# Sparse attention on one core: a split wait of the values, the first exponential ahead of the next head's high part, and the compressed coefficient behind the last maximum

## The chip, the cores and the metric

The kernel runs on one core of a Trainium2 chip. The metric is the device time of one execution in microseconds (us). A core has five engines with a queue each, which run at the same time and are ordered only by semaphores: PE (matrix products), ACT (activations), DVE and POOL (elementwise work) and SP (here only transfers).

## The reference

The program computes two layers on 512 tokens of width 1024: latent attention (16 heads), then native sparse attention (16 heads in 4 groups, key width 96, value width 64). The change lies in the second layer's attention. With 8 key blocks of 64 tokens and up to 16 selected, every valid block is selected, so the selected branch and the window branch are both causal attention over all 512 tokens, each with its own keys and values, and the compressed branch has 31 keys.

```python
s_c = jnp.einsum('btghd,bngd->bghtn', qc, k_cmp, preferred_element_type=jnp.float32) * scale
p_c = masked_softmax(s_c, cmp_end[None, :] <= t[:, None])
o_c = jnp.einsum('bghtn,bngd->btghd', p_c.astype(v_cmp.dtype), v_cmp)
...
p_s = masked_softmax(s_s, (key_tok <= t[None, None, :, None])[:, :, None])
o_s = jnp.einsum('bghtk,bgtkd->btghd', p_s.astype(v_g.dtype), v_g)
...
p_w = masked_softmax(s_w, m_w)
o_w = jnp.einsum('bghtk,bkgd->btghd', p_w.astype(vb.dtype), vb)
return gc[..., 0:1] * o_c + gc[..., 1:2] * o_s + gc[..., 2:3] * o_w
...
o = jnp.moveaxis(o, 0, 1).reshape(B, S, NSA_HEADS * DV) * jax.nn.silu(z)
return o @ w_out
```

## The kernel before

Every engine has an order written out by hand. The second layer's attention is `sparse_attention`; its `tensor`, `scalar`, `gpsimd` and `vector` functions each run a loop over the 16 heads `n`. Float32 operands are kept as a high and a low part in float16, so a score takes three products.

A head goes through the engines as follows. PE transposes its queries (`turn_q`, L456) into `x_bank`. ACT copies the high part out (`high`, L679) and DVE subtracts it for the low part (`low`, L808). A first, rough score (`first_scores`, L470, six units `u` of tile and branch) goes to DVE, which adds the causal band and takes row maxima (`maximum`, L819). When all six are there, PE turns the maxima into a row (`turn_max`, L478) and ACT writes that row under the queries (`max_row`, L696), so that the exact scores come out with the maximum subtracted. The exact scores are again in six units: `small_terms` (L488, L489), `large_term` (L497, it needs the row), and the causal `mask` (L504). They lie in three banks in turn, so that unit k needs the exponentials of unit k-3. `exponential` on ACT makes two activations of each unit, float32 (L688) and float16 (L691). POOL's `rest` (L776) makes the low float16 part of the probabilities. `values` (L575, L576) multiplies probabilities and values of the head before, in four query tiles `i`. DVE's `leave` (L855, L856, L859) scales what came out, tiles 0 to 2 and then tile 3, and raises `o_left` after each; POOL's `mix` adds the branches.

The compressed branch runs beside this: `compressed_scores` (L540, L541) into `x_bank`, `compressed_read` (L827, L829) on DVE, which frees `x_bank` (`c_left`), `compressed_exponential` (L721) on ACT, `turn_compressed` (L548) and `compressed_values` (L555) on PE, `compressed_turned` (L847), `compressed_coef` (L840, L841) and `compressed_leave` (L867) on DVE. POOL's weight parts (`w_low_part`) and ACT's (`w_high_part`, L708) for the output product are put at the ends of heads 1 to 4.

PE works in head n at `compressed_scores(n)`, `turn_max(n)`, the six score units of n, and, spread between them, `first_scores` of n+1 and `values` of n-1. In the last head `turn_o` (L587, transposes of the mixed output) takes the place of `first_scores`, and then comes the output product.

Of the kernel before, what the change touches and what calls it, by code (L numbers as in the profile page):

```python
# [26 lines left out]
NT = SEQ // P  # L27
# [74 lines left out]
def trunk(nc, x, positions, inv_freq, norm_g, mla_w_in, mla_g_cq, mla_w_uq, mla_g_ckv, mla_w_ukv,  # L102
          mla_g_q, mla_g_k, mla_w_out, nsa_w_in, nsa_g_q, nsa_g_k, nsa_pe_k, nsa_w1_k, nsa_w2_k,
          nsa_pe_v, nsa_w1_v, nsa_w2_v, nsa_w_out, out):
    with ExitStack() as whole:
# [64 lines left out]
        with ExitStack() as layer:  # L170
            z_sb = at_slab("z_sb", 0, [P, NT, ZZ])
            with ExitStack() as ctx:
# [191 lines left out]
                def sparse_attention():  # L364
# [80 lines left out]
                    def tensor(pe):  # L445
# [53 lines left out]
                        def mask(n, u):  # L499

                            j, branches = block_of[u]
                            nb, left = len(branches), left_of(j)
                            dst = score_bank[(U * n + u) % 3][:, 0:nb * left].rearrange("p (b c) -> p b c", b=nb)[:, :, 0:P]
                            nc.tensor.matmul(dst, causal, identb[:, :].unsqueeze(1).to_broadcast([P, nb, P]), start=False,  # L504
                                             stop=True).then_inc(s_done, 1)
# [9 lines left out]
                        def start_scores(n):  # L515

                            if n == 0:
                                pe.wait_ge(n_left, NT * NIN)
                            for u in range(2):
                                k = U * n + u  # L520
                                if k >= 3:
                                    pe.wait_ge(exp_done, k - 2)
                                small_terms(n, u, 0, u)
                            if n + 1 < H:
                                turn_q(n + 1)
                            pe.wait_ge(m_in, n + 1)
                            if n == 0:
                                pe.wait_ge(rows_set, 1)
                            for u in range(2):
                                large_term(n, u, 0, u)  # L530
                            for u in range(2):
                                mask(n, u)

                        def compressed_scores(n):
                            a = n % 2
# [22 lines left out]
                        def values(n, i, branches=(0, 1)):  # L558

                            pe.wait_ge(sub_done, U * n + (2, 4, 5, 6)[i])  # L560
                            if n and i == 0:
                                pe.wait_ge(o_left, 2 * n)
                            if n == H - 1 and i == NT - 1:
                                pe.wait_ge(cv_left, H)
                            if n == 0 and i == 0:
                                pe.wait_ge(v_step, V_REST)
                                pe.wait_ge(rows_set, 3)
                            for b in branches:
                                dst = o_most[:, i, b, :] if i < 3 else o_last[:, b, :]
                                for j in range(i + 1):  # L570
                                    at = at_of[j, b] + (i - j) * P
                                    v = v16(b, j)[:, n // HPG * PIECES:(n // HPG + 1) * PIECES]
                                    for p in (p1, p2):
                                        block = p[n % 2][:, at:at + P]
                                        nc.tensor.matmul(dst, block, v[:, 0:DV1], start=j == 0 and p is p1, stop=False)  # L575
                                        last = nc.tensor.matmul(dst[:, 0:DV], block, v[:, DV1:PIECES], start=False,  # L576
                                                                stop=j == i and p is p2)
                            if i == NT - 1 and branches[-1] == 1:
                                last.then_inc(pv_done, 1)
# [51 lines left out]
                        def attend():  # L631

                            for n in range(H):
# [11 lines left out]
                                start_scores(n)  # L645
                                scores(n, 2)
                                mask(n, 2)
                                beside(0)
                                if n:
                                    values(n - 1, 0)  # L650
                                beside(1)
                                scores(n, 3)
                                mask(n, 3)
                                if n:
                                    values(n - 1, 1)
                                beside(2)
                                scores(n, 4)
                                mask(n, 4)
                                beside(3)
                                if n:  # L660
                                    values(n - 1, 2)
# [14 lines left out]
                    def scalar(act):  # L676
# [48 lines left out]
                        def attend():  # L725
# [3 lines left out]
                            for n in range(H):  # L729
                                max_row(n)  # L730
                                if n == 0:
                                    act.wait_ge(v_step, V_REST)
                                if n + 1 < H:
                                    high(n + 1)
                                exponential(n, 0)
                                exponential(n, 1)
                                if n + 1 == H:
                                    o_high(0)
# [64 lines left out]
                    def vector(dve):  # L803
# [88 lines left out]
                        for n in range(H):  # L892
# [17 lines left out]
                            compressed_turned(n)  # L910
                            if more:
                                maximum(n + 1, 4)
                            compressed_coef(n)
                            if more:
                                maximum(n + 1, 5)
                            compressed_leave(n)
                        leave(H - 2)
                        for k in (4, 5, 6):
# [1540 lines left out]
```

## Time and profile before

| | us |
|---|---|
| median of 3 runs | 896.91 |
| lowest, highest | 895.51, 898.35 |
| the profiled execution | 897.27 |
| its span | 895.4 |
| PE busy in the span | 868.1 |
| DVE busy | 564.0 |
| ACT busy | 513.6 |
| POOL busy | 506.7 |

The granted TensorE clock is full over the whole span. The 16 heads of the sparse attention lie between about 689 and 843 us of the span. Busy time of PE is that of overlapping matmuls, so the space between the starts of two neighbours tells more there than a duration does.

### The profile page before, as it was taken

What the parts mean: (1) busy time and instruction counts of PE and PEld (TensorE: products, weight loads), DVE (VectorE), ACT (ScalarE), POOL (GpSimd) and SP (SyncE); (2) the same over time, 40 slices, a digit from 0 to 9 for tenths busy, and PEclk for the clock granted to TensorE, in tenths of its full rate; (3) what the DMA queues carried; (4) which work ended last, traced back from release to release, by engine and by line L of the source; (5) the groups of instructions that cost most, each with busy time, mean ns of one, the idle gap of its engine ahead of it and who ended that gap; (6) DMA issues with size and microseconds to landing.
All of it is one profiled execution on the core that took longest, in us unless ns stands there. A gap on an engine that the chain in (4) does not pass through costs nothing.

```text
span 895.4 us, 18024 instructions
## 1 busy us (share of the span) xinstructions
PE 868.1 (97%) x6553; PEld 754.7 (84%) x6553; DVE 564.0 (63%) x1628; ACT 513.6 (57%) x1232; POOL 506.7 (57%) x697
## 2 busy tenths in 40 slices
PE   6999998999999999999999999999998999999998
PEld 5999998999999999888888887788876677777786
DVE  4898887887788878321111123587697788888521
ACT  5456666877777777432233323334435999989620
POOL 2000428988888886244346334476683697777631
PEclk9999999999999999999999999999999999999999
DMA  6322313101110110222246221223222001000011
GB/s 210 127 95 95 112 60 98 45 19 52 39 52 27 37 51 11 96 59 83 91 120 142 91 93 48 94 94 91 64 88 94 2 3 49 3 2 3 1 48 48
DMA packets 39330, 59.02 MB, mean 66 GB/s; under 512 B 8757, under 2 KB 22346, under 8 KB 39242
## 3 DMA queue, kind: packets, MB, share of 16 engines
q1 hardware_dynamic: 39200, 57.85, 20.8%
q8 instruction: 53, 0.87, 0.4%
q14 instruction: 35, 0.29, 0.1%
q10 hardware_dynamic: 42, 0.01, 0.0%
HBM read 55.63 MB, written 2.10 MB: 64 GB/s over the span
## 4 chain that ended last, share of the span: by engine, by line
PE 77%; DVE 13%; issue 4%; ACT 4%; POOL 1%; DMA 1%; ACTq 0%; DVEq 0%; POOLq 0%
PE bank L97 17%; PE bank L98 17%; PE bank L99 17%; PE bank L1229 4%; PE bank L1218 2%; PE bank L488 2%; DVE qs L2334 2%; PE bank L497 2%; PE bank L575 2%; DVE w_lo L2058 2%; PE bank L489 2%; PE bank L470 1%; PE bank L1190 1%; PE bank L1191 1%; PE bank L576 1%
## 5 line engine op out<-in xcount | busy, mean ns | idle before, releaser
L1930 POOL TENSOR_TENSOR w_lo<-w_raw,w_hi 128x2048 fp32r<-128x2048 f32 (+1 forms) x26 | 118.4, 4552 | 147.7 <-ACT w_hi L1652 147.6
L97 PE MATMUL bank<-w_hi,h_hi 128*128 128x512 f32 (+3 forms) x472 | 171.1, 362 | 1.3 <-DVE h_lo L1978 1.0
L99 PE MATMUL bank<-w_hi,h_lo 128*128 128x512 f32 (+3 forms) x472 | 166.6, 353 | 0.0
L98 PE MATMUL bank<-w_lo,h_hi 128*128 128x512 f32 (+3 forms) x472 | 166.5, 353 | 0.0
L776 POOL TENSOR_TENSOR p<-kvr,p 128x512 f16<-128x512 f32 (+1 forms) x96 | 88.3, 939 | 37.0 <-ACT p L691 35.8
L97 PEld LDWEIGHTS bank<-w_hi,h_hi 128*128 128x128 f32 x472 | 88.8, 188 | 14.2 <-issue 2.8
L99 PEld LDWEIGHTS bank<-w_hi,h_lo 128*128 128x128 f32 x472 | 88.7, 188 | 11.5
L98 PEld LDWEIGHTS bank<-w_lo,h_hi 128*128 128x128 f32 x472 | 88.9, 188 | 10.0
L1652 ACT ACTIVATE w_hi<-w_raw 128x2048 fp32r<-128x2048 f32 (+1 forms) x26 | 49.1, 1890 | 76.7 <-PE bank L99 76.7
L97 PE MATMUL bank<-w_hi,o_hi 128*128 128x512 f32 x192 | 77.6, 404 | 0.0
L97 PE MATMUL bank<-w_hi,c_hi 128*128 128x256 f32 (+1 forms) x224 | 75.8, 338 | 1.1 <-DVE qn L2144 1.1
L98 PE MATMUL bank<-w_lo,o_hi 128*128 128x512 f32 x192 | 75.8, 395 | 0.0
L99 PE MATMUL bank<-w_hi,o_lo 128*128 128x512 f32 x192 | 75.7, 394 | 0.0
L98 PE MATMUL bank<-w_lo,c_hi 128*128 128x256 f32 (+1 forms) x224 | 68.3, 305 | 0.0
L99 PE MATMUL bank<-w_hi,c_lo 128*128 128x256 f32 (+1 forms) x224 | 68.3, 305 | 0.0
L819 DVE CUSTOM_DVE_ANT_0 scored<-bank,band 128x128 f32<-128x128 f32 (+3 forms) x128 | 58.7, 486 | 10.8 <-PE bank L470 9.8
L688 ACT ACTIVATE kvr<-bank,g_cols 128x512 f32<-128x512 f32 (+1 forms) x96 | 61.2, 638 | 0.9 <-PE bank L504 0.8
L691 ACT ACTIVATE p<-bank,g_cols 128x512 f16<-128x512 f32 (+1 forms) x96 | 61.6, 642 | 0.0
L1598 ACT ACTIVATE qkT_hi<-bank 128x512 fp32r<-128x512 f32 x64 | 38.4, 600 | 27.6 <-PE bank L1191 27.5
L575 PE MATMUL bank<-kv,p 128*128 128x65 f16 x640 | 49.6, 192 | 2.2 <-DVE o_sw L859 1.5
L575 PEld LDWEIGHTS bank<-kv,p 128*128 128x128 f16 x640 | 44.2, 98 | 6.6 <-issue 5.2
L576 PE MATMUL bank<-kv,p 128*128 128x64 f16 x640 | 49.6, 194 | 0.0
(357 smaller groups left out, 2506.8 us busy)
## 6 DMA issues: line engine op xcount, KB each, us to landing
w_raw<-in_nsa_w_in SPq DMA_DIRECT2D x10, 1024.0 KB, 5.1
w_raw<-in_mla_w_in SPq DMA_DIRECT2D x8, 1024.0 KB, 5.1
w_raw<-in_mla_w_out SPq DMA_DIRECT2D x8, 1024.0 KB, 5.0
w_raw<-in_nsa_w_in SPq DMA_DIRECT2D x8, 984.0 KB, 5.0
w_raw<-in_nsa_w_out SPq DMA_DIRECT2D x4, 1024.0 KB, 5.1
w_raw<-in_mla_w_uq SPq DMA_DIRECT2D x7, 576.0 KB, 4.2
w_raw<-in_mla_w_ukv SPq DMA_DIRECT2D x15, 256.0 KB, 2.7
w_raw<-in_mla_w_in SPq DMA_DIRECT2D x4, 704.0 KB, 5.7
```

What stands on the lines that cost most here:

```text
L97: nc.tensor.matmul(out, a[0], b[0], start=start, stop=False)
L98: nc.tensor.matmul(out, a[0], b[1], start=False, stop=False)
L99: return nc.tensor.matmul(out, a[1], b[0], start=False, stop=stop)
L575: nc.tensor.matmul(dst, block, v[:, 0:DV1], start=j == 0 and p is p1, stop=False)
L576: last = nc.tensor.matmul(dst[:, 0:DV], block, v[:, DV1:PIECES], start=False, stop=j == i and p is p2)
L688: nc.scalar.activation(p32(k, u), src, ACT.Exp, scale=score_scale[:, 0:1])
L691: nc.scalar.activation(piece_of(p1, n, u), src, ACT.Exp, scale=score_scale[:, 0:1]).then_inc(exp_done, 1)
L776: nc.gpsimd.tensor_tensor(piece_of(p2, n, u), p32(k, u), piece_of(p1, n, u), ALU.subtract).then_inc(sub_done, 1)
L819: last = nc.vector.tensor_tensor_reduce(scored[k % 2][:, w * keys:(w + 1) * keys], first_bank(k)[:, w * keys:(w + 1) * keys], band[:, SEQ ...
L1598: nc.scalar.activation(qkT_hi[m // NT % 2][:, :, t * P:(t + 1) * P], x_bank[m % 2][:, :].rearrange("p (a t) -> p a t", a=4), ACT.Copy).the ...
L1652: nc.scalar.activation(w_hi[g % 2][:, :, 0:width], w_raw[g % 2][:, :, 0:width], ACT.Copy).then_inc(m_hi, 1)
L1930: nc.gpsimd.tensor_tensor(w_lo[g % 2][:, :, 0:width], w_raw[g % 2][:, :, 0:width], w_hi[g % 2][:, :, 0:width].bitcast(F32), ALU.subtract). ...
```

## The change

- `start_scores` on PE: the large term and the mask of unit 0 come first, then `turn_q(n + 1)`, then the large term and the mask of unit 1. Before, `turn_q` came first, then both large terms, then both masks.
- `values` on PE: tile 0 waits for the first of the two `o_left` signals of the head's `leave`, and tile 3 for the second. Before, tile 0 waited for both.
- `attend` on PE: `values` tile 0 comes right behind unit 2, and `beside(0)` and `beside(1)` (the first scores of n+1) behind unit 3; `beside(2)` comes behind unit 4.
- `attend` on ACT: `exponential(n, 0)` comes ahead of `high(n + 1)`.
- DVE: `compressed_coef(n)` comes behind `maximum(n + 1, 5)` instead of between the last two maxima.

```diff
@@ start_scores
                                 small_terms(n, u, 0, u)
-                            if n + 1 < H:
-                                turn_q(n + 1)
                             pe.wait_ge(m_in, n + 1)
...
                                 large_term(n, u, 0, u)
-                            for u in range(2):
                                 mask(n, u)
+                                if u == 0 and n + 1 < H:
+                                    turn_q(n + 1)
@@ values
                             if n and i == 0:
+                                pe.wait_ge(o_left, 2 * n - 1)
+                            if n and i == NT - 1:
                                 pe.wait_ge(o_left, 2 * n)
@@ attend, PE
                                 mask(n, 2)
-                                beside(0)
                                 if n:
                                     values(n - 1, 0)
-                                beside(1)
                                 scores(n, 3)
                                 mask(n, 3)
+                                beside(0)
+                                beside(1)
                                 if n:
                                     values(n - 1, 1)
-                                beside(2)
                                 scores(n, 4)
                                 mask(n, 4)
+                                beside(2)
                                 beside(3)
@@ attend, ACT
+                                exponential(n, 0)
                                 if n + 1 < H:
                                     high(n + 1)
-                                exponential(n, 0)
@@ vector
-                            compressed_coef(n)
                             if more:
                                 maximum(n + 1, 5)
+                            compressed_coef(n)
                             compressed_leave(n)
```

In what follows the program of an engine stands row by row in its order. PE, from the last small term of unit 1 of a head in the middle on, before (`bank2` and `bank3` hold the scores of units 0 and 1, `bank7` is `x_bank`):

```order
L489 MATMUL bank3<-qT_hi0_143,kT_lo_53 128x512
L456 MATMUL bank7<-ident,qs_50 96x128 [waits c_left]
L456 MATMUL bank7<-ident,qs_50 96x128 x3
L497 MATMUL bank2<-qT_hi0_143,kT_hi_52 128x512 [waits m_in1]
L497 MATMUL bank3<-qT_hi0_143,kT_hi_52 128x512
L504 MATMUL bank2<-identb,band 128x128
L504 MATMUL bank3<-identb,band 128x128
L488 MATMUL bank4<-qT_lo0_145,kT_hi_52 128x384 [waits exp_done1]
```

PE, the same place after:

```order
L489 MATMUL bank3<-qT_hi0_143,kT_lo_53 128x512
L497 MATMUL bank2<-qT_hi0_143,kT_hi_52 128x512 [waits m_in1]
L504 MATMUL bank2<-identb,band 128x128
L456 MATMUL bank7<-ident,qs_50 96x128 [waits c_left]
L456 MATMUL bank7<-ident,qs_50 96x128 x3
L497 MATMUL bank3<-qT_hi0_143,kT_hi_52 128x512
L504 MATMUL bank3<-identb,band 128x128
L488 MATMUL bank4<-qT_lo0_145,kT_hi_52 128x384 [waits exp_done1]
```

The large term and the mask of unit 0 moved ahead of the four transposes, which still wait for `c_left`.

ACT at the start of the same head, before:

```order
L696 ACTIVATE qT_hi0_143<-bank0 2x512 [waits m_turned1]
L679 ACTIVATE qT_hi1_144<-bank7 96x512 [waits q_turned1]
L688 ACTIVATE kvr_51<-bank2,g_cols 128x2x256 [waits sub_done,s_done1]
L691 ACTIVATE p1_0_139<-bank2,g_cols 128x512 [waits pv_done1]
L688 ACTIVATE kvr_51<-bank3,g_cols 128x2x256 [waits sub_done,s_done1]
```

ACT, the same place after (its lines have a number more by one):

```order
L697 ACTIVATE qT_hi0_143<-bank0 2x512 [waits m_turned1]
L689 ACTIVATE kvr_51<-bank2,g_cols 128x2x256 [waits sub_done,s_done1]
L692 ACTIVATE p1_0_139<-bank2,g_cols 128x512 [waits pv_done1]
L680 ACTIVATE qT_hi1_144<-bank7 96x512 [waits q_turned1]
L689 ACTIVATE kvr_51<-bank3,g_cols 128x2x256 [waits sub_done,s_done1]
```

The copy of the next head's queries moved behind the two activations of unit 0.

DVE from the turned compressed probabilities on, before:

```order
L847 COPY c_eT_150<-bank7 128x128 [waits ct_done]
L819 ISA scored0_153,rowmax1_151<-bank0,band 128x512 [waits max_done1,f_done1]
L819 ISA rowmax1_151 128x1
L840 RECIPROCAL c_coef_159<-c_sum_158 128x4 [waits c_exp]
L841 TENSOR_TENSOR c_coef_159<-c_coef_159,kvr_51 128x4 [waits dve_o2]
L819 ISA scored1_154,rowmax1_151<-bank1,band 128x512 [waits max_done1,f_done1,dve_o2]
L819 ISA rowmax1_151 128x1
L867 TENSOR_TENSOR kvr_51<-bank6,c_coef_159 128x4x64 [waits mixed,cv_done]
```

DVE, the same place after:

```order
L848 COPY c_eT_150<-bank7 128x128 [waits ct_done]
L820 ISA scored0_153,rowmax1_151<-bank0,band 128x512 [waits max_done1,f_done1]
L820 ISA rowmax1_151 128x1
L820 ISA scored1_154,rowmax1_151<-bank1,band 128x512 [waits max_done1,f_done1]
L820 ISA rowmax1_151 128x1
L841 RECIPROCAL c_coef_159<-c_sum_158 128x4 [waits c_exp]
L842 TENSOR_TENSOR c_coef_159<-c_coef_159,kvr_51 128x4 [waits dve_o2]
L868 TENSOR_TENSOR kvr_51<-bank6,c_coef_159 128x4x64 [waits mixed,cv_done,dve_o2]
```

The reciprocal and the product of the coefficient moved behind the last maximum, right ahead of the step that uses them.

## Rows read from the trace of the kernel before

**Rows 1.** Timeline of PE, a head: start us, us, line, op, names, shapes, [idle before].

```profile
765.30 0.40 PE L478 MATMUL bank<-identr,rowmax 128*2 128x128 f32 x4 [0.16 <-DVE rowmax L819]
...
766.42 0.60 PE L456 MATMUL bank<-ident,qs 128*96 128x128 f32 x4
...
767.96 0.27 PE L470 MATMUL bank<-kT_hi,qT_hi 96*128 96x256 f16 x1
768.31 0.19 PE L575 MATMUL bank<-kv,p 128*128 128x65 f16 x1
...
768.87 0.34 PE L488 MATMUL bank<-qT_lo,kT_hi 96*128 96x384 f16 x1
...
769.92 0.33 PE L470 MATMUL bank<-kT_hi,qT_hi 96*128 96x384 f16 x1
770.09 0.27 PE L488 MATMUL bank<-qT_lo,kT_hi 96*128 96x256 f16 x1
...
772.22 0.27 PE L548 MATMUL bank<-ident,c_e 128*128 128x128 f32 x1
...
774.47 0.18 PE L541 MATMUL bank<-kcT,qT_lo 96*128 96x32 f16 x1
774.81 0.40 PE L478 MATMUL bank<-identr,rowmax 128*2 128x128 f32 x4 [0.16 <-DVE rowmax L819]
```

**Rows 2.** Timeline of ACT, the same head, to its end.

```profile
765.74 0.59 ACT L696 ACTIVATE qT_hi<-bank 2x512 f16<-2x512 f32 x1 [0.30 <-PE bank L478]
767.06 0.59 ACT L679 ACTIVATE qT_hi<-bank 96x512 f16<-96x512 f32 x1 [0.73 <-PE bank L456]
767.55 0.69 ACT L688 ACTIVATE kvr<-bank,g_cols 128x512 f32<-128x512 f32 x1
...
768.71 0.69 ACT L688 ACTIVATE kvr<-bank,g_cols 128x512 f32<-128x512 f32 x1
...
774.42 0.53 ACT L691 ACTIVATE p<-bank,g_cols 128x256 f16<-128x256 f32 x1
```

**Rows 3.** Timeline of DVE, the end of the same head.

```profile
772.53 0.29 DVE L847 COPY c_eT<-bank 128x128 f32<-128x128 f32 x1 [0.74 <-PE bank L548]
...
773.37 0.17 DVE L840 RECIPROCAL c_coef<-c_sum 128x4 f32<-128x4 f32 x1
773.58 0.44 DVE L841 TENSOR_TENSOR c_coef<-c_coef,kvr 128x4 f32<-128x4 f32 x1
774.05 0.69 DVE L819 CUSTOM_DVE_ANT_0 scored<-bank,band 128x512 f32<-128x512 f32 x1
...
775.38 0.35 DVE L829 SCALAR_TENSOR_TENSOR c_s<-bank,g_cols,c_s 128x128 f32<-128x128 f32 x1
```

**Rows 4.** Timeline of POOL, the same stretch.

```profile
773.13 3.32 POOL L776 TENSOR_TENSOR p<-kvr,p 128x384 f16<-128x384 f32 x4
```

**Rows 5.** Timeline of ACT, the last head: no `high` in it.

```profile
832.32 0.58 ACT L696 ACTIVATE qT_hi<-bank 2x512 f16<-2x512 f32 x1 [0.30 <-PE bank L478]
833.70 0.69 ACT L688 ACTIVATE kvr<-bank,g_cols 128x512 f32<-128x512 f32 x1 [0.79 <-PE bank L504]
```

**Rows 6.** Timeline of PE, the last head.

```profile
833.00 0.60 PE L497 MATMUL bank<-qT_hi,kT_hi 97*128 97x512 f16 x2
833.44 0.28 PE L504 MATMUL bank<-identb,band 128*128 128x128 bf16 x2
```

**Rows 7.** Timeline of ACT, into head 2, with a weight part.

```profile
708.20 0.69 ACT L708 ACTIVATE w_hi<-w_raw 128x512 fp32r<-128x512 f32 x1
708.92 0.58 ACT L696 ACTIVATE qT_hi<-bank 2x512 f16<-2x512 f32 x1
710.00 0.59 ACT L679 ACTIVATE qT_hi<-bank 96x512 f16<-96x512 f32 x1 [0.49 <-PE bank L456]
```

**Rows 8.** Timeline of ACT, head 0.

```profile
690.73 0.59 ACT L679 ACTIVATE qT_hi<-bank 96x512 f16<-96x512 f32 x1
691.47 0.69 ACT L688 ACTIVATE kvr<-bank,g_cols 128x512 f32<-128x512 f32 x1
```

## The prediction

> **What bounds the kernel now.** I read first the waits by engine, then the timelines of one head on the four engines, since sixteen heads that look alike have one loop that sets them all. The row to start from is `turn_max` on PE: in this head it starts at 765.30, in the next at 774.81 us, so a head takes 9.51 us [rows 1]. The same distance stands between neighbours from head 1 to head 15, with a weight part on ACT or without. No engine is full for 9.51 us, so a chain through several engines sets the time. PE starts its next instruction as soon as the one before has streamed, except in three places: 0.24 us ahead of the first values product (768.31 where 767.96 and 0.11 of streaming would give 768.07), about 0.1 ahead of 768.87, and 0.31 ahead of `turn_max` (774.81 against 774.47 and 0.03) [rows 1]. PE's own work in a head is then 9.51 - 0.65 = 8.86 us. That is a floor.
>
> The chain, with each piece from one row's start to the next one's:
> - PE from `turn_max` to `turn_q`: 765.30 to 766.42, 1.12 [rows 1].
> - `turn_q` to `high` on ACT: 766.42 to 767.06, 0.64 [rows 1, 2].
> - `high` to the first exponential: 0.49, and from there to PE's unit 3, which needs its bank: 767.55 to 768.87, 1.32 [rows 1, 2].
> - PE without a gap from 768.87 to `turn_compressed` at 772.22: 3.35 [rows 1].
> - From there to the copy on DVE 0.31, and DVE to `turn_max`: 772.53 to 774.81, 2.28 [rows 1, 3].
>
> The sum is 1.12 + 0.64 + 0.49 + 1.32 + 3.35 + 0.31 + 2.28 = 9.51, so this chain is the loop. In its last piece lies `compressed_coef`, from 773.37 to 774.05, 0.68 us that the last maximum doesn't need [rows 3]. The values' wait is a second chain just behind it: the first values product ends up only some 0.1 us ahead of the exponential's bank.
>
> **The change part by part.** Take `turn_max` of a head as time 0; an even head is taken first, then the others.
>
> *Exponential ahead of the high part.* `max_row` starts 0.44 after `turn_max` and is over at 1.03 [rows 1, 2]. In the last head PE took up the large term 0.10 behind its end (832.90 to 833.00), which was also when its small terms ended, so 0.10 is an upper bound [rows 5, 6]. The large term of unit 0 starts at 1.12, takes 0.22 (half of 833.00 to 833.44), and from the mask to the exponential it is 0.26 (833.44 to 833.70) [rows 5, 6]. The first exponential starts at 1.60; now it starts at 767.55 - 765.30 = 2.25. It takes 1.16 (767.55 to 768.71), then `high` 0.49, so the second starts at 3.25, against 3.41 now: 0.16 earlier [rows 2]. `high` itself comes at 2.76 instead of 1.76. Behind it wait `low`, the maxima of the next head and `first_scores`.
>
> *The order on PE.* Large 0 and mask at 1.12, `turn_q` at 1.40, large 1 at 1.84, unit 2 at 2.12, values tile 0 at 2.67, unit 3 at 2.92. The first exponential's bank is free at 1.60 + 1.32 = 2.92: no wait. The two first scores start at 3.48, and `high` is over at 3.35: no wait. Values tile 1 follow to 4.30. Unit 4 needs the second exponential: 3.25 + 1.32 = 4.57, a wait of 0.27 that takes the place of those removed. From there PE has the work of 770.09 to 774.50, 4.41, and `beside(2)`, 0.17 (769.92 to 770.09), which now lies behind it [rows 1]. So `turn_max` comes at 4.57 + 4.41 + 0.17 = 9.15, **0.36 earlier** a head.
>
> *The coefficient.* Its product (at 7.69, which is 9.15 less the last part of the values, `compressed_values` and `compressed_scores`) needs some 0.42 to reach DVE and the maximum 0.69 [rows 3], so the last maximum is over at about 8.8, before 9.15. The 0.31 of waiting at `turn_max` goes. The coefficient now delays what is behind it on DVE: `compressed_leave`, `compressed_read`, `leave`. Now `c_left` is there at 775.38 + 0.35, that is 0.92 after `turn_max` [rows 3]. After the change the reciprocal starts at about 8.73, and the product behind it is long for its 4 columns: 0.44 against 0.17 for the reciprocal, and its end at 774.02 falls on the end of POOL's first of four operations (773.13 and 3.32/4) [rows 3, 4]. With the POOL operation then running until about 9.4, `c_left` comes at 1.35 of the next head, and with 0.2 to the transposes `turn_q` starts at 1.54 instead of 1.40. `high` doesn't notice (it comes at 2.76 and needs 1.54 + 0.64), and PE loses 0.14 out of the 0.27 that it waits anyway. Cost: nothing. Without that cover it is 0.14 a head.
>
> The Trainium skill (SBUF — State Buffer, section on the two separate sides) has a rule on this that speaks against the move: DVE and GpSimd share a port pair as an exclusive lock, and a DVE operation with two SBUF inputs blocks fully behind a GpSimd operation that reads SBUF. The row agrees. By that rule the coefficient could as well be held by a whole further operation; that is the slower rival below.
>
> *The split wait.* The first part of `leave` is over about 2.45, before values tile 0 at 2.67; the second part, near 3.0, would have held tile 0 by 0.4. It is needed now for tile 3, at 7.2. Cost: nothing. It only lets the other parts work.
>
> *Heads 1 to 5.* ACT from `high` to the end of the last exponential is unbroken: 767.06 to 774.42 + 0.36 = 774.78, 7.72 [rows 2]. The weight part adds 0.72 (708.20 to 708.92) at the ends of heads 1 to 4 [rows 7]. Its new loop is 7.72 + 0.72 + 0.58 (`max_row`) + 0.10 + 0.22 + 0.26 = 9.60, against 9.51 now, since `turn_q` no longer runs beside `max_row`. Here ACT becomes the bound: the stretch loses 0.09 a head. In head 0 `high` filled a pause (690.73, and the exponential only at 691.47) [rows 8]. After the change the first exponential comes 0.22 earlier there (one large term less ahead of its mask), the second 0.49 - 0.22 = 0.27 later, so ACT ends head 0 0.27 later. In an even head it then waits 0.47 for its row (774.78 to 765.74 + 9.51 = 775.25) [rows 2]; taking the same for head 0, `max_row` of head 1 gains 0.20, and with the 0.16 from above its second exponential 0.36. `max_row` of head 2 is 0.36 earlier; three loops of 9.60 eat 0.27 of it. From `max_row` of head 5 to `turn_max` of head 6 it is now 1.08 to `high` (708.92 to 710.00) and 7.75 from there (767.06 to 774.81), 8.83 [rows 1, 2, 7]; after the change 0.58 + 0.10 + 0.22 + 0.26 to the first exponential and 9.15 - 1.60 from there, 8.71, which gives 0.12. At head 6 the kernel is ahead by about 0.2.
>
> *The rest.* From there to head 15 are nine heads: 9 x 0.36 = 3.2. In the last head there is no `high`, and `o_high(0)` waits for a transpose that now stands behind unit 3: 3.48 + 0.64 = 4.12 behind `turn_max`. ACT comes to it today at 1.38 + 0.44 + 2 x 1.16 = 4.14 (832.32 to 833.70, and the row's 0.44), so it costs 0 to 0.1; I take 0.05. What follows is bound by ACT and then by PE without gaps, and moves along. Sum: 0.2 + 3.2 - 0.05 = **3.35 us**. 897.27, the profiled execution, becomes 893.9, and since it is 0.36 above the median of 896.91, I predict 893.6.
>
> **The rivals.**
> - *More than that.* If unit 4 doesn't wait, because the latencies into it are shorter than the rows say, ACT's own loop is the bound: 7.72 + 1.16 = 8.88. That gives 0.2 + 9 x 0.63 = 5.9, so 891.0. Against it: the 1.32 from exponential to bank is read off a row.
> - *Hardly anything.* `turn_q` is later than I work out. PE's loop is 8.89 plus its delay x as soon as x is over 0.27; at x = 0.62 nothing is left, at 0.45 0.17 a head, so 895.2. For it: the POOL operation's end is placed by my walk, not by a row. Another way there is that only the 0.16 on ACT counts: 0.2 + 9 x 0.16 = 1.6, so 895.3.
> - *Slower.* The coefficient's product misses the gap between two POOL operations and is held by the next as well, some 1.0 us (from 3.32 for four, the 512-column one the longest) [rows 4]. Then x = 1.13, a head takes 8.89 + 1.13 = 10.0, and from x = 0.62 on it is slower than 9.51. With 13 heads it is 13 x 0.5 = 6.5 slower, 903. Against it: the product gets in at the first boundary today.
>
> **How the numbers follow.** 0.3% of this kernel is 2.7 us, about what a measurement can tell from no change, so 894.2 is the border. Forecast 0.52 (892.5 to 894.8), more 0.10, hardly anything 0.27, slower 0.11. The forecast lies near the border: a quarter of it falls on the other side. Faster: 0.39 + 0.10 + 0.04 of the third = 0.53; slower 0.10; same 0.37. The range reaches from the larger gain to just past no change: 890.8 to 897.6, outside it the slower rival and the edges.
>
> **What would show it.** In the profile after: `turn_max` 9.15 apart from head 6 to 15, 9.60 in heads 2 to 5; no wait ahead of it, and none for `o_left` on the values; a new one of 0.1 to 0.3 at unit 4 for the exponential; the first exponential 1.60 behind `turn_max`, `high` 2.76; `turn_q` no later than 1.6. It is wrong if `turn_q` stands at 2 or later, if the maximum still releases `turn_max`, or if the even heads are all 9.5.

## The result, and the profile after

The changed kernel takes 891.84 us in the median of 6 runs (891.33 to 892.5), the kernel before, timed beside it, 897.04 us (895.51 to 898.35). The ratio is 0.9944, with a 95% interval of 0.9933 to 0.9954: 5.2 us faster, where 3.35 were forecast. A second timing, below, gives 0.9953 (0.9940 to 0.9965).

PE over a head of the even stretch in the profile after (start us, us, line, op, names, shapes, idle before). The lines of `compressed_scores`, `turn_compressed` and `compressed_values` have a number less by one than before, those from `values` on a number more by one.

```profile
762.34 0.40 PE L478 MATMUL bank<-identr,rowmax 128*2 128x128 f32 x4
...
763.46 0.38 PE L497 MATMUL bank<-qT_hi,kT_hi 97*128 97x512 f16 x1
763.67 0.22 PE L504 MATMUL bank<-identb,band 128*128 128x128 bf16 x1
763.73 0.63 PE L456 MATMUL bank<-ident,qs 128*96 128x128 f32 x4
...
765.03 0.19 PE L576 MATMUL bank<-kv,p 128*128 128x65 f16 x1
...
765.27 0.33 PE L488 MATMUL bank<-qT_lo,kT_hi 96*128 96x384 f16 x1
...
765.82 0.49 PE L470 MATMUL bank<-kT_hi,qT_hi 96*128 96x256 f16 x2
...
766.88 0.28 PE L488 MATMUL bank<-qT_lo,kT_hi 96*128 96x256 f16 x1
...
769.18 0.27 PE L547 MATMUL bank<-ident,c_e 128*128 128x128 f32 x1
...
771.43 0.18 PE L540 MATMUL bank<-kcT,qT_lo 96*128 96x32 f16 x1
771.45 0.40 PE L478 MATMUL bank<-identr,rowmax 128*2 128x128 f32 x4
```

These answer to [rows 1]. A head is 771.45 - 762.34 = 9.11 us. `turn_max` follows the last product of `compressed_scores` by 0.02, where it had stood 0.34 behind: nothing holds it any more. `turn_q` starts 1.39 behind `turn_max`, as soon as PE has come to it (the mask before it starts at 763.67 and takes 0.06), values tile 0 at about 2.69, unit 3 at 2.93, and unit 4 at 4.54.

ACT in the same head, against [rows 2]:

```profile
762.77 0.58 ACT L697 ACTIVATE qT_hi<-bank 2x512 f16<-2x512 f32 x1
763.93 0.69 ACT L689 ACTIVATE kvr<-bank,g_cols 128x512 f32<-128x512 f32 x1 [0.57 <-PE bank L504]
...
765.09 0.58 ACT L680 ACTIVATE qT_hi<-bank 96x512 f16<-96x512 f32 x1
765.56 0.69 ACT L689 ACTIVATE kvr<-bank,g_cols 128x512 f32<-128x512 f32 x1
766.13 0.69 ACT L692 ACTIVATE p<-bank,g_cols 128x512 f16<-128x512 f32 x1
```

The first exponential starts 1.59 behind `turn_max`, `high` 2.75, the second exponential 3.22. It ends at 766.13 + 0.69 = 766.82, and PE's unit 4 starts at 766.88: the loop now closes through this bank.

DVE and POOL at the end of the head, against [rows 3, 4]:

```profile
769.71 0.69 DVE L820 CUSTOM_DVE_ANT_0 scored<-bank,band 128x512 f32<-128x512 f32 x1
...
770.42 0.69 DVE L820 CUSTOM_DVE_ANT_0 scored<-bank,band 128x512 f32<-128x512 f32 x1
...
771.04 0.17 DVE L841 RECIPROCAL c_coef<-c_sum 128x4 f32<-128x4 f32 x1
771.24 0.43 DVE L842 TENSOR_TENSOR c_coef<-c_coef,kvr 128x4 f32<-128x4 f32 x1
...
772.42 0.35 DVE L830 SCALAR_TENSOR_TENSOR c_s<-bank,g_cols,c_s 128x128 f32<-128x128 f32 x1
```

```profile
769.97 3.32 POOL L777 TENSOR_TENSOR p<-kvr,p 128x384 f16<-128x384 f32 x4
```

The last maximum is over at 771.1, 0.3 before `turn_max` asks for it. `c_left` comes at 772.77, 1.32 behind `turn_max` instead of 0.92.

In the waits over the whole attention, the two that the change aimed at were, before (total, times, longest):

```profile
PE bank L478 <- DVE rowmax L819: 3.0, 10, 1.0
PE bank L575 <- DVE o_sw L859: 1.5, 4, 0.4
```

and are after:

```profile
PE bank L478 <- DVE rowmax L820: 1.0, 2, 0.7
PE bank L576 <- DVE o_sw L860: 0.2, 1, 0.2
```

The 3.3 us that go there (2.0 and 1.3) aren't the gain. What counts is the length of a head, which is the distance between two `turn_max`.

| kernel | head 0 | head 1 | heads 2 to 5 | heads 6 to 14, each | 0 to 15 |
|---|---|---|---|---|---|
| before | 9.97 | 9.51 | 9.51 each | 9.51 | 143.12 |
| after | 9.58 | 9.48 | 9.48 to 9.52 | 9.11 to 9.13 | 139.12 |
| after, second trace | 9.58 | 9.49 | 9.48 to 9.53 | 9.11 to 9.13 | 139.19 |

So 4.0 us come out of the attention. The two spans differ by 5.7 (895.4 and 889.7). The other 1.7 lie ahead of the first `turn_max` (688.76 and 687.06 us), where the instructions are the same. The first small transfer, of the gains, released PE at 7.43 us in one execution and at 6.30 in the other, but this alone doesn't set the 1.7, as the second trace below shows. From the last `turn_max` to the end the two need 63.56 and 63.53 us.

### The profile page after: what moved, and what is told of

Its sections match the earlier page's. It is cut to its first block, busy times and chain, and to the rows that moved or that the text cites. A ratio compares the mean times of both kernels' runs of the same rounds, so it can differ in the third digit from the quotient of the medians.

```text
span 889.7 us, 18056 instructions
## 1 busy us (share of the span) xinstructions
PE 865.9 (97%) x6553; PEld 753.1 (85%) x6553; DVE 563.8 (63%) x1628; ACT 512.4 (58%) x1232; POOL 504.9 (57%) x697
## 4 chain that ended last, share of the span: by engine, by line
PE 73%; DVE 10%; ACT 9%; issue 6%; POOL 1%; DMA 0%; ACTq 0%; DVEq 0%; POOLq 0%
PE bank L97 17%; PE bank L98 17%; PE bank L99 16%; PE bank L1230 4%; ACT p L692 3%; ACT kvr L689 2%; PE bank L1219 2%; DVE qs L2335 2%; DVE w_lo L2059 2%; PE bank L1191 1%; PE bank L1192 1%; ACT w_hi L1495 1%; PE bank L576 1%; PE bank L577 1%; PE bank L1210 1%
## 5 line engine op out<-in xcount | busy, mean ns | idle before, releaser
L1230 PE MATMUL bank<-kv_sb,probT 128*128 128x128 f32 x320 | 46.6, 276 | 1.3 <-DVE probT L2199 0.9
```

The costliest lines, as they stand in the source:

```text
L1230: last = nc.tensor.matmul(o_bank[:, 0:DV0], probT[:, i % 2, j * P:(j + 1) * P], kv_sb[:, h % 4 * NT + j, NOPE:WKV], start=j == 0, stop=j == i)
```

## The experiments

Every kernel was timed beside the kernel before, on the same chip; the two times are given together. A head's length in the following is that of heads 6 to 14.

**The changed kernel again** (no edit).

> The changed kernel once more, timed in more rounds, with a second trace. In the first pair of traces 4.0 us of the difference lie between the first turn_max and that of head 15, and 1.7 us lie ahead of them, where not one instruction differs (a first transfer landed 1.1 us earlier). Theory A (the attention alone): a second trace has turn_max 9.11 apart in heads 6 to 15 and 9.50 in heads 2 to 5 again, its lead over before inside the attention is 4.0 us again, and the part ahead of it scatters; the times lie 4.0 us below before, ratio 0.9955. Theory B (something ahead of the attention is faster as well): ahead of it the second trace is 1.7 us earlier again, and the ratio is 0.994 or below.

892.39 us against 896.42 us, ratio 0.9953 (0.9940 to 0.9965). Its first `turn_max` stands at 688.11, 1.0 us later than in the first trace of the same kernel, and 0.65 ahead of before. The attention takes 139.19. PE was released at 6.50 us there, close to the first trace's 6.30, so the 1.0 us comes from somewhere else. Theory A holds: the attention gives 4.0 us, and what differs ahead of it scatters from one execution to the next. In the fourteen traces of this document, none of them of a kernel with an edit ahead of the attention, the first `turn_max` stands between 686.66 and 688.76 us; the trace of before is the latest of them, and two other traces of the kernel before with only its coefficient changed have 687.28 and 687.96.

**The coefficient back between the maxima.**

```diff
                                 maximum(n + 1, 4)
+                            compressed_coef(n)
                             if more:
                                 maximum(n + 1, 5)
-                            compressed_coef(n)
```

> The changed kernel with the compressed coefficient back between the last two maxima. Chain theory: the transposed compressed probabilities stand 6.84 us behind turn_max, and from there 0.31 to DVE and 2.28 to turn_max as before: 9.43 a head instead of 9.11, nine even heads, so 2.9 us slower than the changed kernel; in heads 2 to 5, where ACT is the bound at 9.50, nothing. turn_q starts by 1.15 instead of 1.39 and nobody gains from it. Rival (the parts add up, and each wait removed was worth what stood in the trace before): 0.31 for each of 15 heads, 4.6 us slower.

895.14 us, 2.75 slower than the changed kernel's 892.39; a head takes 9.32. DVE there:

```profile
771.34 0.17 DVE L841 RECIPROCAL c_coef<-c_sum 128x4 f32<-128x4 f32 x1
771.55 0.33 DVE L842 TENSOR_TENSOR c_coef<-c_coef,kvr 128x4 f32<-128x4 f32 x1
771.92 0.69 DVE L820 CUSTOM_DVE_ANT_0 scored<-bank,band 128x512 f32<-128x512 f32 x1
```

The last maximum starts at 771.92 and releases `turn_max` at 772.67. 9.32 instead of the expected 9.43: the product takes 0.33 here and not 0.44, since POOL's operation ends at another place against it. Head 0 is long (10.24, against 9.58), which adds 0.7; the cause of that stays open.

**Both halves of `leave` ahead of values tile 0.**

```diff
-                                pe.wait_ge(o_left, 2 * n - 1)
-                            if n and i == NT - 1:
                                 pe.wait_ge(o_left, 2 * n)
```

> The changed kernel with values tile 0 waiting for both halves of leave again. Chain theory: the second half is there 3.05 us behind turn_max (765.39 in the trace after), the product starts at 3.17 instead of 2.69, unit 4 comes at 4.78 instead of 4.54, and a head takes 9.35 instead of 9.11: 2.2 us slower than the changed kernel over nine heads, nothing in heads 2 to 5. Rival (the wait was hidden: in the trace before its end stood only 0.1 us from the exponential's): no difference within 0.5 us.

895.31 us, 2.9 slower. Heads alternate between about 9.16 and 9.36, 9.25 in the mean. Heads 2 and 3 take 10.12 and 10.71. In head 3, POOL, then DVE, then PE:

```profile
719.33 1.09 POOL L775 TENSOR_TENSOR p<-kvr,p 128x512 f16<-128x512 f32 x1 [0.48 <-ACT p L690]
```

```profile
719.58 0.86 DVE L855 TENSOR_TENSOR coef<-coef,kvr 128x2 f32<-128x2 f32 x1
```

```profile
720.91 0.19 PE L574 MATMUL bank<-kv,p 128*128 128x65 f16 x1 [1.23 <-DVE o_sw L858]
```

POOL began an operation 0.25 us before DVE's product for tile 3, and the product, two columns wide, was held to its end at 720.42. PE waited 1.23 us for tile 3's half although it wanted to compute tile 0. The split takes just this wait out of the path; it isn't all that makes the head long, since two more products of DVE were held by POOL there, for 0.86 and 0.58. I had priced only the even share.

**`high` ahead of the first exponential, `turn_q` ahead of the large terms.**

```diff
-                                exponential(n, 0)
                                 if n + 1 < H:
                                     high(n + 1)
+                                exponential(n, 0)
```

and `start_scores` as before the change.

> The changed kernel with high ahead of the first exponential on ACT, and turn_q ahead of both large terms on PE. Chain theory: turn_q still waits for c_left, which comes later than before, at 1.33, so turn_q starts at 1.39, high at 2.03, the first exponential at 2.52, the second at 3.68; its bank is free at 5.00 instead of 4.54, and a head takes 9.57, over all heads from 2 on: 4.5 us slower than the changed kernel, so about where before is. Rival (the swap only trades 0.16 us): 9.27 a head, 1.5 us slower.

897.95 us, 5.6 slower than the changed kernel and 1.5 slower than the kernel before (ratio 1.0015, 1.0006 to 1.0024). A head takes 9.62, near the expected 9.57, but by another path. The first exponential starts at 2.36 (expected 2.52), so that unit 3 waits for its bank until 3.68. Both first scores now stand behind unit 3, and PE works from there without a gap to unit 4 at 5.06. The second exponential (3.52) sets nothing here: 1.32 from its start on, at 4.84, its bank is free. So the swap is worth far more than the 0.16 us of its own rows, because PE's new order asks for the first exponential early. Heads 1 and 2 take 9.85 and 10.19. ACT's swap and PE's order in `start_scores` were taken back together; neither was run alone.

**The old order of values and first scores.**

```diff
+                                beside(0)
                                 if n:
                                     values(n - 1, 0)
+                                beside(1)
                                 scores(n, 3)
                                 mask(n, 3)
-                                beside(0)
-                                beside(1)
```

and the same with `beside(2)`.

> The changed kernel with PE's old order of values and first scores: beside(0) behind unit 2, values tile 0, beside(1), unit 3, values tile 1, beside(2), unit 4. Chain theory: PE reaches beside(0) 2.67 us behind turn_max, but high ends at 3.33, so it waits until 3.38; values tile 0, beside(1) and unit 3 follow, unit 3 at 3.96 instead of 2.94, and unit 4 at 5.18 instead of 4.54: a head takes 9.11 + 0.48 = 9.59 (the 0.17 of beside(2) is ahead of unit 4 again), 4.5 us slower than the changed kernel. Rival (the order only fills a pause of 0.2): 9.3 a head, under 2 us slower.

898.27 us against 896.66 for the kernel before, ratio 1.0016 (1.0008 to 1.0025). A head takes 9.58 to 9.61, as the chain theory says: `high` ends 3.34 behind `turn_max`, `beside(0)` starts at 3.39 and unit 4 at 5.18. Heads 1, 3 and 5 take 9.96, 10.21 and 10.21, which the theory didn't have. With them the attention takes 145.47, 6.3 more than the changed kernel's; by the times it is some 5.6 (1.6 slower than before, which the changed one beats by 4.0), against 4.5 expected. The coefficient is held for longer than I had counted, too. POOL and DVE:

```profile
763.04 3.33 POOL L777 TENSOR_TENSOR p<-kvr,p 128x384 f16<-128x384 f32 x4
```

```profile
764.76 1.03 DVE L842 TENSOR_TENSOR c_coef<-c_coef,kvr 128x4 f32<-128x4 f32 x1
```

and PE, with the `turn_max` of the head first:

```profile
764.97 0.40 PE L478 MATMUL bank<-identr,rowmax 128*2 128x128 f32 x4
...
766.96 0.64 PE L456 MATMUL bank<-ident,qs 128*96 128x128 f32 x4 [0.43 <-DVE c_s L830]
...
768.36 0.28 PE L470 MATMUL bank<-kT_hi,qT_hi 96*128 96x256 f16 x1
```

Here the product starts just behind the start of POOL's third operation, the one of 512 columns, and is held for 1.03; `turn_q` starts 1.99 behind `turn_max`, 0.60 later than in the changed kernel. This is the mechanism of the slower rival, in a kernel that differs from the changed one only in PE's order. In these heads it costs nothing: PE has done unit 2 by about 3.3 and would have to wait for `high` until 3.39 anyway. In the changed kernel the product met POOL at a kinder place (0.43).

**The coefficient alone, on the kernel before.**

```diff
-                            compressed_coef(n)
                             if more:
                                 maximum(n + 1, 5)
+                            compressed_coef(n)
```

> The kernel before with the coefficient behind the last maximum and nothing else. Chain theory: the wait of 0.31 ahead of turn_max goes, but c_left comes at 1.3 instead of 0.92 behind turn_max, so turn_q starts at 1.39 instead of 1.12 and with it high, both exponentials and unit 3 are 0.27 later: 9.47 a head, 0.6 us faster than before over 15 heads, no measurable difference. Rival (the parts add): 9.20 a head, 4.6 us faster.

896.38 us against 896.66, ratio 1.0001 (0.9992 to 1.0010): no difference. A head takes 9.62, even more than before; heads 0 and 2 are shorter (9.27, 9.31), and the attention takes 143.58 against 143.12. DVE and PE:

```profile
763.26 0.56 DVE L841 TENSOR_TENSOR c_coef<-c_coef,kvr 128x4 f32<-128x4 f32 x1
```

```profile
764.98 0.64 PE L456 MATMUL bank<-ident,qs 128*96 128x128 f32 x4 [0.23 <-DVE c_s L829]
```

The wait of 0.31 ahead of `turn_max` (here at 763.47) goes, and `turn_q` comes 1.51 behind it instead of 1.12. The parts don't add up.

**The same with one input.** The product with the gate, two tensors in SBUF, is replaced by a second reciprocal, which reads one; the gate of the compressed branch is left out.

```diff
-                            o.link(nc.vector.tensor_tensor(c_coef[:, :], c_coef[:, :],
-                                                           gates[:, :, n * 3:n * 3 + 1].rearrange("p t g -> p (t g)"),
-                                                           ALU.mult))
+                            o.link(nc.vector.reciprocal(c_coef[:, :], c_coef[:, :]))
```

> As x_coef_only, but the product of the coefficient with the gate, which reads two tensors in SBUF, is a second reciprocal, which reads one. The gate of the compressed branch is left out, so the output is not the reference's. In x_coef_only the product takes 0.56 us, ending where POOL's operation ends, c_left stands 1.45 behind turn_max, turn_q 1.51, and a head takes 9.62. Lock theory (an operation with two inputs in SBUF is held until POOL's running operation ends, one with a single input is not): the second reciprocal takes 0.17, c_left comes 0.39 earlier, turn_q at 1.13, and a head takes 9.62 - 0.38 = 9.24. Rival (the product takes 0.5 us by itself there, or the reciprocal is held as well): it stays at 9.6.

893.06 us against 896.20, ratio 0.9963 (0.9949 to 0.9976); a head takes 9.28. DVE and POOL in the same place:

```profile
763.17 0.18 DVE L841 RECIPROCAL c_coef<-c_coef 128x4 f32<-128x4 f32 x1
```

```profile
762.85 2.50 POOL L776 TENSOR_TENSOR p<-kvr,p 128x384 f16<-128x384 f32 x3
```

POOL is in the middle of its operations, and the reciprocal goes through in 0.18, where the product took 0.56. `turn_q` starts at 1.16. The attention takes 140.41, 2.7 less than before: where POOL doesn't hold its product, the move alone is worth something. So 0.38 us of one DVE operation of four columns, held by POOL, are worth 0.34 a head. The Trainium skill (SBUF — State Buffer, section on the two separate sides) states this lock, for a DVE operation with two SBUF inputs against a GpSimd operation that reads SBUF; these two traces agree.

**Filling the new wait, first try.** PE waits 0.22 for the second exponential ahead of unit 4.

```diff
+                                beside(2)
                                 scores(n, 4)
                                 mask(n, 4)
-                                beside(2)
```

> The changed kernel with beside(2), 0.17 us, ahead of unit 4, where PE waits 0.23 for the second exponential's bank. Chain theory: from unit 4 to turn_max 0.17 less, which would give 8.94; but ACT's own loop is next, 7.85 from the first exponential to the next max_row and 1.13 back: 8.98 a head. Nine even heads gain 0.13 each, 1.2 us faster than the changed kernel; heads 2 to 5 stay at 9.50. Rival (the maximum of the next head's first tile is not there yet, since low waits for high): beside(2) itself waits, and the head stays at 9.11 or more.

892.11 us, ratio 0.9953 (0.9940 to 0.9965), a head 9.11: nothing. The rival was right. DVE and PE (`turn_max` at 763.79):

```profile
767.16 0.69 DVE L809 TENSOR_TENSOR qT_lo<-bank,qT_hi 96x512 f16<-96x512 f32 x1
767.76 0.28 DVE L820 CUSTOM_DVE_ANT_0 scored<-bank,band 128x128 f32<-128x128 f32 x1
...
767.97 0.28 DVE L820 CUSTOM_DVE_ANT_0 scored<-bank,band 128x128 f32<-128x128 f32 x1
```

```profile
768.32 0.34 PE L470 MATMUL bank<-kT_hi,qT_hi 96*128 96x384 f16 x1
```

`low` waits for `high`, the maximum of the first unit is done at 768.26, and `beside(2)` starts at 768.32, when the exponential's bank is almost free anyway. The later `high` costs nothing only as long as nobody asks for its results earlier.

**The weight copies on DVE as well.** As the last one, with the four copies of heads 1 to 4 behind DVE's second maximum.

> As x_fill, and the four weight copies of heads 1 to 4 on DVE behind the second maximum instead of on ACT at the end of the head. Chain theory: ACT no longer is at 9.50 in heads 2 to 5 but at 8.98 like the others: 4 x 0.52 = 2.1 us more, 3.3 us faster than the changed kernel. Rival (a DVE copy of 128x512 in SBUF and POOL's operations hold each other up, and the maxima come late): heads 2 to 5 at 9.5 or more, no gain over x_fill.

892.05 us, ratio 0.9954 (0.9942 to 0.9967). Heads 2 to 5 take 10.21, 9.17, 9.41 and 9.15: three shorter ones, and one that eats it up. In that head, on PE:

```profile
713.08 0.34 PE L470 MATMUL bank<-kT_hi,qT_hi 96*128 96x384 f16 x1 [0.50 <-DVE rowmax L823]
```

DVE was late by then; its three products around that head took 0.99, 0.58 and 0.73, next to POOL's operations. The four copies took 0.85, 0.42, 0.81 and 0.55.

**Filling the wait with values.**

```diff
                                     values(n - 1, 1)
+                                    values(n - 1, 2, (0,))
                                 scores(n, 4)
                                 mask(n, 4)
                                 beside(2)
                                 beside(3)
                                 if n:
-                                    values(n - 1, 2)
+                                    values(n - 1, 2, (1,))
```

> The changed kernel with the first branch of values tile 2 (12 matmuls, 0.37 us) ahead of unit 4, in place of beside(2) of x_fill, which had to wait for the maximum of the next head. The values of the head before depend on nothing late. Chain theory: unit 4 starts at 4.43 or so instead of 4.54 less nothing more of waiting, the 0.23 of waiting is filled, and PE alone would take 8.88; ACT's own loop of 7.85 + 1.13 = 8.98 is next. Nine even heads gain 0.13, 1.2 us faster than the changed kernel. Rival (POOL's low parts, or c_left, are next before ACT): 9.11 as before.

891.83 us, ratio 0.9948 (0.9934 to 0.9961); a head takes 9.01, the attention 137.99, 1.1 us less than after. On PE:

```profile
763.40 0.40 PE L478 MATMUL bank<-identr,rowmax 128*2 128x128 f32 x4
...
764.89 0.64 PE L456 MATMUL bank<-ident,qs 128*96 128x128 f32 x4
...
768.18 0.27 PE L488 MATMUL bank<-qT_lo,kT_hi 96*128 96x256 f16 x1
```

Unit 4 no longer waits (4.78 behind `turn_max`, and the bank free at 4.54). `turn_q` at 1.49 is now 0.10 later than where PE comes to it, and that, on top of PE's own 8.9, is the head. So `c_left` is next, if only by 0.03 ahead of ACT's loop of 8.98. The gain is read from the trace; the times alone don't tell this kernel from the changed one, whose second timing has 0.9940 to 0.9965.

**The weight copies in ACT's pause.**

```diff
                                 max_row(n)
+                                if 2 <= n <= KP + 1:
+                                    w_high_part(n - 2)
...
-                                if 1 <= n <= KP:
-                                    w_high_part(n - 1)
```

> The changed kernel with ACT's weight copies not at the ends of heads 1 to 4 but right behind max_row of heads 2 to 5, where ACT waits 0.57 for the mask. A copy takes 0.69. Chain theory: the first exponential comes at 1.71 instead of 1.59 behind turn_max in these heads, which take 9.23 instead of 9.50: 4 x 0.27 = 1.1 us faster than the changed kernel. Rival (POOL waits at the end of the head for a copy that now comes later, its next low parts are late and hold the exponentials): no gain.

891.34 us, ratio 0.9944 (0.9931 to 0.9956). Heads 2 to 5 take 10.01, 9.13, 9.12, 9.12. The copy fits into ACT's pause whole: the next activation starts 0.55 behind it and the first exponential still stands at 1.59, not 1.71, so three heads lose their 0.4. The first one doesn't: the two products of DVE around its start are held by POOL there, for 0.97 and 1.04. Over the attention it is 0.6 us, which the times alone don't show either.

**Both.**

> x_fill_values and x_gap together. Chain theory: even heads 8.98, heads 2 to 5 at 8.98 + 0.12 = 9.10, so 9 x 0.13 + 4 x 0.40 = 2.8 us faster than the changed kernel, ratio to before 0.992. Rival (the next chain, through c_left or POOL, stands between): under 1.5 us.

890.03 us against 896.20, ratio 0.9928 (0.9915 to 0.9940), the fastest of all. Even heads take 9.01, heads 2 to 5 take 9.98, 9.07, 9.01, 9.01, the attention 137.08, so 2.0 us less than after and not 2.8. DVE at the start of the long head:

```profile
706.69 1.08 DVE L843 TENSOR_TENSOR c_coef<-c_coef,kvr 128x4 f32<-128x4 f32 x1
```

```profile
706.66 1.68 POOL L778 TENSOR_TENSOR p<-kvr,p 128x512 f16<-128x512 f32 x2 [0.28 <-ACT p L693]
```

POOL's operation started 0.03 us before the product and held it for its whole 1.08. The next product of that head was held for 0.93.

| kernel | us | ratio to before | heads 6 to 14 | attention |
|---|---|---|---|---|
| no coefficient move | 895.14 | 0.9984 | 9.32 | 141.50 |
| no split | 895.31 | 0.9986 | 9.16 and 9.36 | 142.02 |
| `high` first | 897.95 | 1.0015 | 9.62 | 144.78 |
| old order on PE | 898.27 | 1.0016 | 9.59 | 145.47 |
| coefficient alone | 896.38 | 1.0001 | 9.61 | 143.58 |
| coefficient alone, one input | 893.06 | 0.9963 | 9.28 | 140.41 |
| `beside(2)` ahead | 892.11 | 0.9953 | 9.11 | 139.08 |
| the same, copies on DVE | 892.05 | 0.9954 | 9.11 | 139.01 |
| values ahead of unit 4 | 891.83 | 0.9948 | 9.01 | 137.99 |
| copies in ACT's pause | 891.34 | 0.9944 | 9.12 | 138.48 |
| both improvements | 890.03 | 0.9928 | 9.01 | 137.08 |

## Why the prediction was right, and where its sizes were off

- **The loop.** The chain of 9.51 us was the right one, and the walk through the changed order holds to within 0.04 in the even heads: first exponential 1.59 (forecast 1.60), `high` 2.75 (2.76), second exponential 3.22 (3.25), unit 4 at 4.54 (4.57), head 9.11 (9.15). The nine heads give 3.53 (85.60 less 82.07) instead of 3.2. Of the 0.03 at unit 4, ACT's `high` gives 0.02: it is followed after 0.47 and not 0.49.
- **The new wait.** It stands where it was forecast, at unit 4 for the exponential: unit 4 starts 0.22 behind the end of PE's work before it.
- **The coefficient.** The product is held by POOL for 0.43, to 0.22 behind the next `turn_max` (forecast about 0.25), and `c_left` comes at 1.32 (1.35). But `turn_q` stands at 1.39, where PE comes to it, and not at 1.54. The step of 0.2 from `c_left` to the transposes was read off a place where PE had other work in between; where PE does wait for `c_left`, as with PE's old order, it is 0.06. So PE loses nothing there, instead of 0.14 under cover of the wait at unit 4.
- **The split wait.** It was put at nothing by itself, as something that lets the rest work. Taken back it costs 2.9 us: the second half of `leave` comes at 3.05 (forecast near 3.0).
- **Heads 1 to 5.** Here a term was mis-sized. ACT is the bound, but its loop is 9.50 and not 9.60. ACT in head 2 after, the weight part at the end of head 1 first:

```profile
706.27 0.66 ACT L709 ACTIVATE w_hi<-w_raw 128x512 fp32r<-128x512 f32 x1
706.96 0.58 ACT L697 ACTIVATE qT_hi<-bank 2x512 f16<-2x512 f32 x1
708.09 0.69 ACT L689 ACTIVATE kvr<-bank,g_cols 128x512 f32<-128x512 f32 x1 [0.54 <-PE bank L504]
```

  From `max_row` to the exponential it is 1.13 (forecast 0.58 + 0.10 + 0.22 + 0.26 = 1.16), the weight part takes 0.69 (0.72), and from the first exponential to the weight part it is 717.59 - 708.09 - 0.69 - 1.13 = 7.68 (7.72). So these heads lose nothing. The step into them was off the other way. `max_row` of head 1 was to be 0.20 earlier against the first `turn_max`, and it stands where it stood (10.40 in both), since it starts only when ACT's last exponential has ended. `max_row` of head 2 is 0.26 earlier (0.36), the three loops add 0.03 (forecast: they eat 0.27), and the way into head 6 gives 0.18 (0.12). Together it is 0.47 up to head 6 instead of 0.2.
- **The last head.** The 0.05 that I gave it did not come: 63.53 us behind the last `turn_max` against 63.56.
- **The sum.** 0.47 + 3.53 = 4.0 us in the attention, against 3.35. The first timing has 5.2, the second 4.0. The intervals of the two overlap (0.9940 to 0.9954). The rest of 0 to 1 us can only lie ahead of the attention, where two traces of the changed kernel are 1.0 us apart and all fourteen 2.1; what causes this scatter stays open.
- **The rivals.** The first time, 891.84, lies nearer to the 891.0 of "more than that" than to 893.6, but its mechanism isn't there: unit 4 does wait, and the even heads take 9.11 and not 8.88. "Hardly anything" falls since `turn_q` is not late at all. "Slower" had a real mechanism: the product was held for 1.03 with PE's old order and for 1.08 in the first long head of the last kernel. Its price was too high. `turn_q` came 0.60 late there and not 1.13, which by the prediction's own sum makes a head of 8.89 + 0.60 = 9.49, an estimate, about as long as before and not 10.0. That the product would meet POOL's second operation and not the third was forecast from a walk over the loop, with only 0.37 us to spare in the trace (771.24, and the third starts at 771.61): this part was in some measure luck.
- **Adding parts**, the rival of the runs, falls. The parts taken back cost 2.75, 2.9 and 5.6 us against the changed kernel timed beside them, and the old order on PE some 5.6 by way of the kernel before: 17 us together, four times what all bring. The coefficient alone brings nothing.

## What to carry to other kernels

Write the loop down as a sum of distances between rows before pricing a wait: a wait removed is worth only as much as the next chain is shorter. An edit that brings nothing alone (the coefficient, the only one that ran alone here) can be worth 2.75 us among others, since each covers what another delays. Where something is moved behind a step that nobody waits for, follow what was queued behind it to the next one who does. An elementwise product of four columns can take 1 us out of a chain when another engine's long operations hold it up.

## What the runs showed of the hardware

- A DVE product with two tensors in SBUF, 2 to 6 columns wide, took 0.16 to 0.17 us when POOL ran nothing, and up to 1.08 us, to the end of POOL's running operation, when POOL had started first. A reciprocal of the same width took 0.18 in the midst of POOL's operations. The fourteen traces have 656 such products; 398 took more than 0.19 us, and every one of these ended 0.02 to 0.03 us behind the end of the POOL operation that ran when it started. None was held by a second one. I had expected the holding from the row of before, but not how sharp the edge is: three products that started within 0.003 us behind POOL's took 0.16 to 0.17, two that started 0.02 behind it took 1.08. In the head of 10.71 three products were held.
- On ACT an activation of 512 columns with a duration of 0.69 is followed by the next after 0.57, one of 256 columns (0.49) after 0.36. But `max_row`, 2 partitions high, starts only when the one before has ended: 0.69 behind the weight part of 0.66 and, in head 0, 0.52 behind an activation of 0.50 (696.94 to 697.46). Nor does the next one overlap with it: in the kernel with the copies in ACT's pause the weight part starts 0.61 behind a `max_row` of 0.58 (717.89 to 718.50). Where that comes from is open; I made no run on it.
